# Transposing the normalised activations with DMA crossbar transposes instead of TensorE, in a hybrid encoder layer on eight cores

## The reference, cut to what matters

```python
def rmsnorm(x, g):
    y = x * rsqrt(mean(x * x, axis=-1) + 1e-6)
    return y * g

h = rmsnorm(x, g_mix)                       # shared by all mixers
q, k, v, f = split(h @ w_in, [1024, 2048, 3072], axis=-1)   # 3584 columns in all
q, k = rope(rmsnorm(q, g_q)), rope(rmsnorm(k, g_k))         # 16 maps of 64 columns
a = softmax(q1 k1 / 8) - lam * softmax(q2 k2 / 8)           # differential, 8 heads
attn = (rmsnorm(a @ v, g_sub) * 0.8) @ w_attn_br
four = real(fft2(f)) @ w_four_br                            # over tokens and 128 channels, 4 groups
gates = sigmoid(h @ w_gate + b_gate)
x1 = x + (gates[0] * attn + gates[1] * four) @ w_out
h2 = rmsnorm(x1, g_mlp)
y = x1 + square(relu(h2 @ w_up)) @ w_down                   # hidden width 4096
```

## Time and profile before

| | |
|---|---|
| median of 3 runs | 5367.49 us |
| profiled execution: span of the slowest core (core 5) | 5410.9 us |
| spans of the other cores in it | 5353.2 to 5406.6 us |
| mean granted TensorE clock, die 0 and die 1 | 0.966 and 0.957 |
| busy: TensorE, ScalarE, VectorE, GpSimd | 92%, 49%, 35%, 10% of the span |
| stage A of the first, second, third sequence (first norm to last projection) | about 93, 73 and 71 us |
| attention of one sequence with its projections | about 895 us |
| one quarter of stages C and D | about 185 us, 12 of them |

### The profile page before, as it was taken

The page is one execution under the profiler, slowest core; times in us unless marked ns, Lnnn a source line. Parts: engine busy times, 40 slices in busy tenths (PEclk is TensorE's granted clock), DMA queues, the critical chain, the costliest instruction groups (busy, mean ns, idle before and its releaser), DMA issues.

```text
span 5410.9 us, 65888 instructions; the slowest of 8 cores (5353.2 to 5410.9 us)
## 1 busy us (share of the span) xinstructions
PE 4968.2 (92%) x27036; PEld 1957.4 (36%) x27036; DVE 1877.2 (35%) x2569; ACT 2624.5 (49%) x3410; POOL 547.3 (10%) x577
## 2 busy tenths in 40 slices
PE   4999989999999899998998999999999989899998
PEld 2333323334444443332223444444233322344443
DVE  2344344432232234435343223214444444412321
ACT  2487678821121238867783122123787678412211
POOL 1122231100000011112110000000111121000000
PEclk9999999999999999999999999999999999999999
DMA  9411176035444430000003535443000000244553
GB/s 148 94 22 18 22 83 76 8 133 177 149 164 165 156 94 9 5 5 15 8 8 118 177 137 168 165 159 114 9 5 5 9 15 8 103 162 149 171 173 125
DMA packets 158812, 477.56 MB, mean 88 GB/s; under 512 B 53552, under 2 KB 91568, under 8 KB 129584
## 3 DMA queue, kind: packets, MB, share of 16 engines
q1 hardware_dynamic: 82272, 389.46, 20.9%
q0 software_dynamic: 76240, 83.89, 9.3%
HBM read 481.71 MB, written 58.72 MB: 100 GB/s over the span
## 4 chain that ended last, share of the span: by engine, by line
PE 71%; ACT 12%; DVE 7%; issue 6%; DMA 3%; POOL 1%; ACTq 0%; DVEq 0%; SPq 0%; POOLq 0%
PE pall L232 70%; ACT sb_ov L247 11%; DVE sb_ov L250 3%; DVE sb_ov L262 3%; DMA sb_ov<-x 2%; POOL sb_ov L250 1%; DMA sb_wst<-wb_mix 1%; DVE sb_ov L253 1%; DVE sb_ov L256 1%; DMA wb_vf<-w_in 1%; PE pall L234 0%; ACT sb_sm L247 0%; PE pall L237 0%; ACT L247 0%; ACTq L129 0%
## 5 line engine op out<-in xcount | busy, mean ns | idle before, releaser
L247 ACT ACTIVATE sb_ov<-pall 128x1024 bf16<-128x1024 f32 (+1 forms) x2232 | 1952.1, 888 | 1193.9 <-PE pall L232 1121.6
L232 PE MATMUL pall<-sb_ov 128*64 128x512 bf16 (+1 forms) x6144 | 1518.5, 403 | 59.0 <-ACT sb_ov L247 34.2
L232 PE MATMUL pall<-sb_wst,sb_ov 128*128 128x512 bf16 x4608 | 1009.9, 380 | 12.9 <-DVE sb_ov L250 8.6
L234 PE MATMUL pall<-sb_ov 128*64 128x512 bf16 x3072 | 992.9, 402 | 0.0
L232 PE MATMUL pall<-sb_ov,sb_cmat 128*64 128x512 bf16 (+1 forms) x2064 | 779.6, 393 | 132.8 <-ACT sb_ov L247 49.7
L232 PEld LDWEIGHTS pall<-sb_ov 128*64 128x64 bf16 (+1 forms) x6144 | 367.7, 101 | 1070.1 <-issue 772.4
L232 PE MATMUL pall<-sb_ov,sb_wst 128*128 128x512 bf16 x3072 | 722.0, 402 | 31.5 <-DVE sb_ov L250 31.5
L232 PE MATMUL pall<-sb_hT,sb_wst 128*128 128x512 bf16 x3072 | 713.6, 382 | 2.8 <-DVE sb_frT L250 2.8
L250 DVE TENSOR_TENSOR sb_ov<-sb_ov 128x512 bf16<-128x512 bf16 (+2 forms) x864 | 455.8, 537 | 632.2 <-ACT sb_ov L247 575.1
L232 PEld LDWEIGHTS pall<-sb_wst,sb_ov 128*128 128x128 bf16 x4608 | 448.1, 98 | 559.0 <-DVE sb_ov L250 14.5
L250 DVE TENSOR_TENSOR sb_ov<-pall,sb_ov 128x512 f32<-128x512 f32 x384 | 253.9, 687 | 1011.8 <-PE pall L232 666.5
(11 more groups left out here) (54 smaller groups left out, 2215.5 us busy)
## 6 DMA issues: line engine op xcount, KB each, us to landing
sb_wst<-wb_up SPq DMA_DIRECT2D x96, 1024.0 KB, 5.8
sb_wst<-wb_down SPq DMA_DIRECT2D x96, 1024.0 KB, 5.8
sb_wst<-wb_mix SPq DMA_DIRECT2D x96, 896.0 KB, 5.4
sb_ov<-x SPq DMA_DIRECT2D x48, 512.0 KB, 4.1
sb_ov<-x POOLq DMA_DIRECT2D x12, 2048.0 KB, 25.6
sb_wst<-wb_out SPq DMA_DIRECT2D x24, 1024.0 KB, 5.8
y<-sb_ov POOLq DMA_DIRECT2D x12, 2048.0 KB, 11.4
sb_wst<-dftc SPq DMA_DIRECT2D x12, 1024.0 KB, 6.7
```

Source lines behind the costliest of these rows:

```text
L232: P.op("pe", lambda e: e.matmul(out, lhsT=lhsT, rhs=rhs, start=start, stop=stop), reads, writes)
L234: P.op("pe", lambda e: e.matmul(out, lhsT=lhsT, rhs=rhs, start=start, stop=stop, tile_position=tp), reads, writes)
L247: P.op("act", lambda e: e.activation(out=out, in_=in_, func=func, **kw), reads, writes)
```

## The change

The normalising multiplication takes g_mix (later g_mlp) as a third operand, from a float32 copy of it that is the same on all partitions. Two sets of gains share one place in `ov` (`O_GB`, column 39936), which the attention's third `O_PT` buffer uses as well, so g_mix is loaded at the start of each sequence and g_mlp ahead of stage C, 512 KB each, on SP's queue. The transposes of a tile are one `dma_start_transpose` of 128x1024 bf16, issued on SP's queue, from `hb` or `hb2` straight into `hT` or `O_H2T`; the 768 TensorE transposes and the 96 operations of VectorE that emptied them are gone. What was TensorE's and VectorE's wait for `hb` becomes a wait on SP's queue.

```diff
--- before.py
+++ after.py
@@ -166,6 +166,7 @@
     w_up_d = din("w_up", [1024, 4096], F32)
     w_down_d = din("w_down", [4096, 1024], F32)
     vecs_d = din("vecs", [128, 36], F32)
+    gb_d = din("gb", [128, 2, DM], F32)
     lams_d = din("lams", [128, 4, 64], F32)
     cmat_d = din("cmat", [128, 8, 128], BF16)
     rope_d = din("rope", [128, 2, SEQ], F32)
@@ -207,9 +208,9 @@
         wst = [sb("wst%d" % i, [128, 4096], BF16) for i in range(NWST)]
         ov = sb("ov", [128, OVN], BF16)
 
-        ident, blk, rotm, ones, onesm, ccm, nscm, esel = [cmat[:, i, :] for i in range(8)]
+        _, blk, rotm, ones, onesm, ccm, nscm, esel = [cmat[:, i, :] for i in range(8)]
         cosT, sinT = rope[:, 0, :], rope[:, 1, :]
-        gm, gmlp, bg = vecs[:, 0:8], vecs[:, 8:16], vecs[:, 16:32]
+        bg = vecs[:, 16:32]
         gq, gk, gsub = vecs[:, 32:33], vecs[:, 33:34], vecs[:, 34:35]
         epsc = sm[:, 0:1]
         neglam = sm[:, 1:2]
@@ -233,8 +234,8 @@
             else:
                 P.op("pe", lambda e: e.matmul(out, lhsT=lhsT, rhs=rhs, start=start, stop=stop, tile_position=tp), reads, writes)
 
-        def TR(out, in_, reads, writes):
-            P.op("pe", lambda e: e.transpose(out, in_, ident), reads + ["cmat"], writes)
+        def XBT(out, in_, slot, reads, writes):
+            P.dma("sp", lambda e: e.dma_start_transpose(out=out, in_=in_), slot, reads=reads, writes=writes)
 
         def ACT(out, in_, func, reads, writes, bias=None, scale=None, accum_out=None):
             kw = {}
@@ -366,18 +367,22 @@
         O_HB2 = (32768, 33792)
         O_DT = (34816, 36864)
         O_RL = (38912, 39424)
-        gm_bc = gm.unsqueeze(2).to_broadcast([128, 8, 128])
-        gmlp_bc = gmlp.unsqueeze(2).to_broadcast([128, 8, 128])
 
         def rms_rstd(ss_col, rs_col, reads, tagw):
             ACT(sm[:, rs_col:rs_col + 1], sm[:, ss_col:ss_col + 1], AF.Ln, reads + ["sm_eps"], [tagw + "ln"], bias=epsc, scale=1.0 / DM)
             ACT(sm[:, rs_col:rs_col + 1], sm[:, rs_col:rs_col + 1], AF.Exp, [tagw + "ln"], [tagw], scale=-0.5)
 
+        O_GB = 39936
+
+        def load_gain(i, slot):
+            DMA("sp", ovf(O_GB, 2048), gb_d[:, i, :], slot, [], ovc(O_GB, 2048))
+
         def hT_res(tc):
             return [("hT", tc * 4 + i) for i in range(4)]
 
         for s in range(nseq):
             r0 = s * SEQ
+            load_gain(0, ("gm", s))
             bV = wload(s, wb_vf[0], 4096, R_VFA)
             bF = wload(s, wb_vf[2], 4096, R_VFA)
 
@@ -389,18 +394,13 @@
                 DMA("sp", xa, x_d[r0 + t * 128:r0 + (t + 1) * 128, :], ("xa", i, s), [], c_xa)
                 ACT(hb, xa, AF.Square, c_xa, c_hb + [("ssx", i)], accum_out=sm[:, 10 + i:11 + i])
                 rms_rstd(10 + i, 12 + i, [("ssx", i)], "rsx%d" % i)
-                TS1(hb, xa, sm[:, 12 + i:13 + i], ALU.mult, c_xa + ["rsx%d" % i], c_hb)
+                STT(hb, xa, sm[:, 12 + i:13 + i], ovf(O_GB, 2048), ALU.mult, ALU.mult, c_xa + ["rsx%d" % i] + ovc(O_GB, 2048), c_hb)
 
             def a0_tr(t):
                 i = t % 2
                 hb = ovb(O_HB[i], 1024)
                 c_hb = ovc(O_HB[i], 1024)
-                b = nb()
-                pt = bank(b).bitcast(BF16)
-                for j in range(8):
-                    TR(pt[:, j * 128:(j + 1) * 128], hb[:, j * 128:(j + 1) * 128], c_hb, [bres(b)])
-                TT(hT[:, :, t * 128:(t + 1) * 128], pt.rearrange("p (j t) -> p j t", j=8), gm_bc, ALU.mult,
-                   [bres(b), "vecs"], [("hT", t)])
+                XBT(hT[:, :, t * 128:(t + 1) * 128], hb, ("xt", i, s), c_hb, [("hT", t)])
 
             def vproj(t, bw, dst_lo, eng):
                 b = nb()
@@ -669,6 +669,7 @@
                 DMA("sp", dbg_frT, frT[:], "dbg2", [("frT", g, tq) for g in range(4) for tq in range(NTC)], ["dbg2"])
             while late_list:
                 late_list.pop(0)()
+            load_gain(1, ("gl", s))
             NHOIST = 2
 
             def mix_step(tc, j, s=s):
@@ -711,18 +712,15 @@
                     c_hb2 = ovc(O_HB2[i], 1024)
                     ACT(hb2, ovf(xo, 2048), AF.Square, ovc(xo, 2048), c_hb2 + [("ssy", i)], accum_out=sm[:, 14 + i:15 + i])
                     rms_rstd(14 + i, 16 + i, [("ssy", i)], "rsy%d" % i)
-                    TS1(hb2, ovf(xo, 2048), sm[:, 16 + i:17 + i], ALU.mult, ovc(xo, 2048) + ["rsy%d" % i], c_hb2)
+                    STT(hb2, ovf(xo, 2048), sm[:, 16 + i:17 + i], ovf(O_GB, 2048), ALU.mult, ALU.mult,
+                        ovc(xo, 2048) + ["rsy%d" % i] + ovc(O_GB, 2048), c_hb2)
 
                 def d_tr(tt):
                     i = tt % 2
                     hb2 = ovb(O_HB2[i], 1024)
                     c_hb2 = ovc(O_HB2[i], 1024)
-                    b = nb()
-                    pt = bank(b).bitcast(BF16)
-                    for j in range(8):
-                        TR(pt[:, j * 128:(j + 1) * 128], hb2[:, j * 128:(j + 1) * 128], c_hb2, [bres(b)])
                     h2v = ovb(O_H2T, 4096).rearrange("p (j t) -> p j t", j=8)[:, :, tt * 128:(tt + 1) * 128]
-                    TT(h2v, pt.rearrange("p (j t) -> p j t", j=8), gmlp_bc, ALU.mult, [bres(b), "vecs"], ovc(O_H2T, 4096))
+                    XBT(h2v, hb2, ("yt", i, s), c_hb2, ovc(O_H2T, 4096))
 
                 for tt in range(4):
                     for ch in range(2):
@@ -832,11 +830,12 @@
     vecs[:, 32] = np.tile(g_q, 2)
     vecs[:, 33] = np.tile(g_k, 2)
     vecs[:, 34] = g_sub
+    gb = np.ascontiguousarray(np.broadcast_to(np.stack([g_mix, g_mlp])[None], (128, 2, DM))).astype(np.float32)
     lams = np.ascontiguousarray(np.broadcast_to(np.stack([lq1, lk1, lq2, lk2])[None], (128, 4, 64))).astype(np.float32)
     shared = {
         "w_in": np.ascontiguousarray(w_in), "w_gate": np.ascontiguousarray(w_gate), "w_attn": np.ascontiguousarray(w_attn),
         "w_four": np.ascontiguousarray(w_four), "w_out": np.ascontiguousarray(w_out), "w_up": np.ascontiguousarray(w_up),
-        "w_down": np.ascontiguousarray(w_down), "vecs": vecs, "lams": lams, "cmat": cmat, "rope": rope,
+        "w_down": np.ascontiguousarray(w_down), "vecs": vecs, "gb": gb, "lams": lams, "cmat": cmat, "rope": rope,
         "dftc": dftc, "dfts": dfts, "nyq": nyq,
     }
     in_maps = [dict(shared, x=np.ascontiguousarray(x)) for x in xs]
```

## The result

The changed kernel takes **1.017 times** the time of the kernel before, 95% interval 1.0145 to 1.0194: about +91 us, 5459 us on the 5367.5 us of before. The medians of the five runs of each, 5588.58 against 5440.12 us, hold runs in which the chip granted one die a lower clock; the ratio leaves these out, and as the trace of before has a little of it on die 1, where the core of the earlier trace rows sits, stages are compared on die 0. So it is slower, beyond its interval, and inside my range, but within 2%, where I had put 0.43, and not on the side with 0.55. The profiled execution took 5453.69 us.

A forecast was written before the change was run, and what follows sets the result against it. TensorE was taken as the bound (71% of the chain), except loads of x in the first sequence's stage A. Terms 20 + 15 + 56 + 25 = +116 us on the 5367.5 us median gave 5484 us, 2.2% slower, range 5385 to 5700 us.

The forecast's parts named there:

- the side with 0.55: Whole kernel slower by more than two percent (107 us): chance 0.55, against 0.43 within 2% and 0.02 faster.
- What bounds the kernel, and what is removed: 96 transposed tiles at 0.45 us leave TensorE: 43 us, 0.8% of the span, all that can be won directly.
- The price of a transpose: On SP's queue, 2.4 us fixed plus 3.2 us for 1024 pieces at 49 ns: 5.6 us; SP held 1.2 us.
- The transposes in line, each behind the landing of the one before: After the out projection four transposes run one after another with SP waiting, issued from 1153.4, the last landing at 1176.
- the light rival: Transposes land in 3.3 us, hold SP 0.33 us and do not queue: +44 us, 5411 us; chance 0.27.
- Quarters 0 to 2: Out projection, nine times: the mix load behind the third transpose leaves TensorE standing 13 us; +6.3 us each, +56 us.
- Fourth quarter: Out projection, three times, no mix step as cover: `wb_up` load behind the last transpose; +8.4 us each, +25 us.
- Stage A: Second and third sequence: 4.5 us a tile where TensorE had 3.90, +10 us twice; first sequence +15 us.
- The gains: Loading g_mix and g_mlp costs nothing, 3 us to spare before the first mix step; uncovered, up to 5 us, three times.
- The heavy one: Rival: every transpose lands in 11.7 us, +435 us in all, 5803 us; chance 0.17.
- the one of single elements: Rival: the DMA moves 2-byte elements instead of crossbar blocks, 40 us a transpose, +1500 us and more; chance 0.02.
- the faster one: Rival: all waits are covered and the 43 us come back, 5324 us; chance 0.02.

The follow-up runs named there:

- the hybrid with separate resources: The hybrid with a resource of its own for each of the last three transposed tiles of a quarter; 5287.49 and 5290.43 us, ratio 0.9863.
- early loads: Changed kernel with g_mlp's load behind the first three mix loads and weight loads issued ahead of stage D's first and third transposes; ratio 0.9973.
- the hybrid: The kernel with early loads, but x in stage A transposed on TensorE and multiplied by g_mix while emptied; only x1 on the crossbar; ratio 0.9881.
- the gains alone: Changed kernel with both transposes back on TensorE, emptied by a plain copy, gains still folded into the normalising instruction; 5384.72 to 5387.33 us, +22 us.
- run 6: Not a follow-up run: in "those run 6 us after the last products" the word is a verb, said of the attention's last `sb_dm` matmuls.

## Why the prediction came out as it did

**What bounds the kernel, and what is removed**: the pace was right, 0.45 us a tile, and in the changed kernel another wait ends later in each place where that time was freed. That these 43 us are all that can be won was wrong. TensorE also stood idle around the transposes, 135.7 us before them in all (57 us of it until the first tile of all was ready), and the hybrid with separate resources won back 77 us with half of the tiles. I had priced only TensorE's own work and not the waits that leave with it.

**The price of a transpose: wrong, and the step that failed.** I put 5.6 us together from 2.4 us fixed and 49 ns for each of 1024 pieces. The count was right: the hardware queue has 102240 more packets than before (184512 against 82272), 98304 of them 96 x 1024. The price per piece was not. That queue's share of the engines rose from 20.9% of 5410.9 us to 23.5% of 5452.1 us, 2406 us of engine time, under 25 ns a packet even with the gain loads in it.

```profile
q1 hardware_dynamic: 184512, 417.79, 23.5%
```

The 49 ns were those of another queue's converting packets in a crowded stretch, and both count: on core 0 of the changed kernel, from 57 to 113 us, the converting packets took 45 ns and the transposes' packets of the same 256 bytes 36 ns, and these took 22 ns from 1200 to 1800 us (means). In that first stretch the transposes really land late, the first six in 10.5 to 14.3 us, twice my 5.6; elsewhere in 3.1. I had the nearer row, equal bytes on the same queue at 3.3 us, and used it as a lower end only. The Trainium skill, Advanced Engine Details and Errata, section on X-Bar Transpose, says that on trn2 a transposing DMA is as fast as a regular one. Outside the crowded stretch the trace agrees, 3.1 against 3.3 us. The 1309 ns a block of the Trainium skill, VectorE: DVE Perf Modes, section on the three transpose paths, does not add up over a wide transpose: eight blocks landed in 3.1 us and four in 2.5. SP's hold, 1.2 us, and the multiplication, 1.28 us, came out as 1.23 and 1.285 us.

```profile
L254 DVE SCALAR_TENSOR_TENSOR sb_ov<-sb_ov,sb_sm 128x1024 bf16<-128x1024 f32 x96 | 123.3, 1285 | 286.9 <-ACT sb_sm L248 286.9
```

**The transposes in line, each behind the landing of the one before**: a step that followed from the wrong price. At 3.1 us the first three are done before the next norm is, as the light rival said; SP waits for VectorE, not for a landing. The kernels with early loads show the line once a landing takes 6 to 8 us, and the run with separate resources shows what it costs in the hybrid, some 1.3 us a quarter in the hoist.

**Quarters 0 to 2**: mechanism right, size too large, +38 us for +56 us. The mix load behind the third transpose and its stand of TensorE were as told (11.5 us for 13). The load itself took 6.7 us where I had 5.9, with the next load and a transpose beside it. And TensorE came back at the lower of its two levels (1.2 GHz, a granted clock of 0.50 from 1193 on in the gap and in the four microseconds that hold the first matmuls after it, 1.00 from 1208 on), which cost 2.1 us a quarter in the hoist, as told; but the kernel before had paid only 1.0 us for its own gap on die 0, not the 2 us of the core I read, so less was won back. That difference is 1 us a quarter of loss; without it the term would have been further off. That the cause is the order on SP's queue and not the transposes is shown by the run with early loads. Columns of the window: its length, busy time and instructions of each engine, granted clock, DMA share, GB/s.

```profile
1200.00:1204.00 4.00, 3.11 (x8) 1.20 (x9) 0.00 (x0) 0.00 (x0) 0.00 (x0) 0.50 1.14 346
...
1208.00:1215.00 7.00, 7.00 (x34) 3.21 (x33) 2.31 (x4) 2.06 (x3) 0.00 (x0) 1.00 0.41 150
```

**Fourth quarter**: +13 us for +25 us, the same wrong line of transposes; the last one was issued at 1758.0, as soon as its norm was ready.

```profile
1757.96 1.23 SPq L238
...
1759.29 5.04 DMA sb_wst<-wb_up
```

**Stage A**: +8 us for +20 us in the later two (+9 without the down projections that the row holds). The cycle of the two buffers was told rightly (hold, load of x, norm), but x landed mostly in 3.5 to 5 us where the term had 4.6, and the transpose was out of the way in 3.1. The recorded start, tile 2's norm done at 1866.1, is also 0.5 us early by the prediction's own terms (1863.6 + 1.16 + 0.6 + 1.3 = 1866.7), which changes the term by 1 us. The chain:

```profile
1914.47 1.23 SPq L238
...
1915.80 3.80 DMA sb_ov<-x
...
1919.73 1.16 ACT sb_ov L248 x2
...
1921.29 3.57 DMA sb_ov<-x
```

In the first sequence the loss was there (+11 us for +15), yet in another place: before the first projection, where the first transpose lands after 12.45 us among the conversions and TensorE had taken 1 us. Some 2 us of it are the folded gains' own: with the gains alone the first projection starts at 62.9 us, against 61.0 and 71.5.

```profile
58.02 12.45 DMA sb_hT<-sb_ov
...
70.60 4.42 PE pall L233 x10
```

**The gains: "nothing, with 3 us to spare" was wrong**, +18 us. I had named the third `O_PT` buffer as what `O_GB` shares. It also shares columns 39936 to 40959, which are `O_FIN + 3072` and `+ 3584`, the two operands that the attention's last `sb_dm` matmuls read, and those run 6 us after the last products. So the three mix loads start when they are already due, and land together in 9.7 us:

```profile
1113.86 0.64 PE L235 MATMUL pall<-sb_ov,sb_dm 128*64 128x512 bf16 x1
...
1115.02 2.49 SPq L269 DMA_DIRECT2D sb_wst<-wb_mix  x3
...
1124.74 1.89 PE L233 MATMUL pall<-sb_oT,sb_wst 128*128 128x512 bf16 x4 [7.66 <-DMA sb_wst<-wb_mix]
```

I had kept "up to 5 us, three times" for the case that the cover goes; it was 6.0 us.

**The rivals.** The light rival had the price of a transpose and the time of the line right, and with SP's hold at 1.23 us (0.9 us more in 12 quarters) and the gain load's 18 us added it gives 44 + 11 + 18 = 73 us of the 89 measured; of the rest some 10 us lie in stage A and 7 in quarters 0 to 2. The heavy one, the one of single elements and the faster one are out for this kernel. The sum's errors lay on both sides: four terms were together 46 us too large and one 18 us too small, so that 1.017 came near 1.022 partly by luck.

## What to carry to other kernels

When a step moves to a DMA queue, the price is mostly what stands behind its wait: list the loads that follow it on that queue and issue those that need not wait ahead of it; here that, with the gain load moved, turned 1.7% slower into no slower (0.997) with all 96 transposes in place, and into 1.4% faster with the 48 of stage D alone, each with a resource of its own. Before placing a new buffer over an old one, look up every reader of each of its cells, also the late ones of the stage's tail. Take a price from the same queue in a stretch as crowded as the one it is for: here the same packet took 36 ns in one and 22 in the other. And when work leaves an engine, count also the waits that stand around it.

## What the runs showed of the hardware

- A crossbar transpose of 128x1024 bf16 from SBUF to SBUF landed in 3.0 to 3.1 us when nothing was ahead of it, moved 1024 packets of 256 bytes, and held SP's queue for 1.23 us; one of 512 columns held it for 1.25 us and landed in 2.5 us. With 1.9 MB of plain loads just ahead of it, it landed in 6.6 us (median of 36, 5.8 to 9.2), and beside the conversions on POOL's queue in 10.5 to 14.3 us.
- A plain load issued right behind a transpose held SP for 0.53 us (median) instead of 0.33.
- Emptying a PSUM bank of 128x1024 bf16 took VectorE 0.68 us as a copy and 1.22 us with a broadcast operand.
- A TensorE gap of 11.5 us cost 2.1 us afterwards at the lower clock level; one of 3 us before the up projection cost 1.0 us (medians of die 0 in nine quarters).
